# Moving half of the sample-state updates of each mLSTM head into the next head

## The reference, cut to what matters

```
num = einsum(s, v) + w_inter * einsum(q, c_st)          # each of the 4 tokens reads the old memory
den = sum(s) + w_inter * einsum(q, n_st)
h   = num / max(|den|, exp(-m_t))
c_new = decay * c_st + einsum(w_row, k, v)              # the memory that is written back
hn  = (h - mean(h)) * rsqrt(var(h) + EPS)               # per-head norm
out = (hn + skip * xc) * silu(z)
```

## Time and profile before

| | us |
|---|---|
| median of three runs | 1763.48 |
| the profiled execution's own time | 1764.59 |
| its span | 1762.6 |
| TensorE busy in it | 1609.9 (91%) |
| VectorE busy | 665.3 (38%) |
| ScalarE busy | 389.7 (22%) |
| GpSimd busy | 221.7 (13%) |
| DMA, mean over the span | 103 GB/s |

### The profile page before, as it was taken

How to read it: one execution, slowest core, us unless ns; L and a number is a source line. 1 busy time by engine, 2 the same in 40 slices (tenths; PEclk the granted TensorE clock), 3 DMA queues, 4 the chain that set the end, 5 groups by cost and what they waited for, 6 DMA issues and landing times. The chain is left out here.

```text
span 1762.6 us, 22229 instructions
## 1 busy us (share of the span) xinstructions
PE 1609.9 (91%) x8553; PEld 1084.1 (62%) x8553; DVE 665.3 (38%) x1418; ACT 389.7 (22%) x916; POOL 221.7 (13%) x293
## 2 busy tenths in 40 slices
PE   6998598989898699997995999999899999999987
PEld 5886264646464598443444998894347775477752
DVE  1542225555454731005113222032205762176624
ACT  3211131313141321004002221210003331133202
POOL 4010040303030000000003110000201112011120
PEclk9998888989999799998997999959999999999999
DMA  5110027474747622123824240021312211222011
GB/s 161 56 41 0 5 90 244 149 256 145 250 159 242 233 96 103 56 95 125 264 73 135 88 138 1 5 96 48 94 59 97 73 30 52 92 77 77 3 67 51
DMA packets 92639, 181.89 MB, mean 103 GB/s; under 512 B 9927, under 2 KB 23907, under 8 KB 91331
## 3 DMA queue, kind: packets, MB, share of 16 engines
q1 hardware_dynamic: 89286, 163.76, 27.6%
q0 software_dynamic: 3248, 16.72, 2.9%
HBM read 133.82 MB, written 54.95 MB: 107 GB/s over the span
## 5 line engine op out<-in xcount | busy, mean ns | idle before, releaser
L1112 PE MATMUL ps<-wring,xnT 128*128 128x512 f32 (+2 forms) x464 | 177.9, 546 | 0.0
L1112 PEld LDWEIGHTS ps<-wring,xnT 128*128 128x128 f32 (+1 forms) x464 | 83.3, 196 | 97.0 <-issue 96.9
L347 PE MATMUL ps<-xnT,wring 128*128 128x288 f32 (+1 forms) x512 | 120.6, 397 | 1.2 <-PEq L2395 1.2
L1112 PE MATMUL ps<-wring,xcT 128*128 128x512 f32 x256 | 110.9, 594 | 0.0
L347 PEld LDWEIGHTS ps<-xnT,wring 128*128 128x128 f32 x512 | 98.0, 193 | 20.9 <-ACT xnT L268 1.3
L884 DVE SCALAR_TENSOR_TENSOR wring<-wring,nbw,ps 128x512 f32<-128x512 f32 x128 | 86.7, 742 | 63.3 <-PE ps L635 62.1
L2033 ACT ACTIVATE P<-ps,nmx 128x128 f32<-128x128 f32 (+3 forms) x128 | 67.3, 527 | 168.1 <-DVE nmx L2057 167.1
L1932 PE MATMUL ps<-KT,Qp 128*128 128x128 f32 (+3 forms) x256 | 96.5, 459 | 0.0
L2057 DVE TENSOR_REDUCE nmx<-ps 128x1 f32<-128x128 f32 (+3 forms) x128 | 62.0, 486 | 85.2 <-PE ps L1933 84.9
L1112 PEld LDWEIGHTS ps<-wring,xcT 128*128 128x128 f32 x256 | 48.3, 190 | 62.6 <-issue 62.6
L1997 PE MATMUL ps<-V,PT 128*128 128x64 f32 x640 | 85.1, 265 | 0.0
(11 more groups left out here) (434 smaller groups left out, 2755.7 us busy)
## 6 DMA issues: line engine op xcount, KB each, us to landing
wring<-in_state_C_dram SPq DMA_DIRECT2D x32, 1024.0 KB, 6.0
out_dram<-wring SPq DMA_DIRECT2D x32, 1024.0 KB, 5.6
wring<-in_a_w_up_dram SPq DMA_DIRECT2D x8, 2048.0 KB, 8.9
wring<-in_b_w_in_dram SPq DMA_DIRECT2D x8, 2048.0 KB, 8.2
wring<-in_a_w_down_dram SPq DMA_DIRECT2D x4, 2048.0 KB, 7.8
craw<-in_cache_kv_dram SPq DMA_DIRECT2D x64, 128.0 KB
arena<-in_cache_kv_dram SPq DMA_DIRECT2D x32, 256.0 KB, 3.8
arena<-in_cache_win_dram SPq DMA_DIRECT2D x8, 1024.0 KB, 4.9
```

Source lines behind the costliest of these rows:

```text
L347: m = pe.matmul(b[:, 0:t1 - t0], w[:, kt, 128 * m4:128 * m4 + 128], k.xnT[:, kt, t0:t1], start=kt == 0, stop=kt == KD - 1)
L1112: m = pe.matmul(b[0:n, 0:w.shape[2]], xT[:, 8 * half + kt, 128 * i:128 * i + n], w[:, kt, :], start=half == 0 and kt == 0, stop=half == ha ...
```

## The change: what it does

States 4 to 7 of a head (`LATE = 4`) are no longer read and updated within the head but in the first part of the next one: state 4 behind the K products, 5 behind the value products, 6 behind the token-major keys, 7 behind the scores. State 3 moves from ahead of the output products to behind the first transposes that follow them. The fold of the samples' reads ("nums") follows state 7 in the next head; the samples' own product goes into `acc` ahead of the first state's read, and their row sums ("dens") behind the fourth memory product. The samples' variance, deviation and norm move accordingly: the deviation behind the fourth memory product's copy on ScalarE, the norm behind the copy of the row sums on VectorE. For this the halves `kS`, `vS` and the decay rows `nbw` get two buffers, used by turns, and GpSimd waits for state 7 of the head before ahead of the spread queries. The last head has no next one: its states 4 to 7 come at the end of the cell. To make room, the scans' two constant rows lie in the second half of the weight ring and are set in `stage_gates` instead of in the input norm. The core of the diff:

```diff
+LATE = 4
-    nbw = sb("nbw", [128, 2 * S + SB])
+    nbws = sb("nbw", [128, 2, 2 * S + SB])
-    kS = sb("kS", [128, AD], F32R)
-    vS = sb("vS", [128, AD], F32R)
+    kSs = sb("kS", [128, 2, AD], F32R)
+    vSs = sb("vS", [128, 2, AD], F32R)
...
 # sample_state, ahead of state 0
+            pe.wait_ge(k.p_ready, 5 * h + 5)
+            pe.matmul(acc[0:S, :], pS[:, :], vt[0:S, NT, :], start=True, stop=False)
...
+    def sum_samples(pe, h):
+        pe.wait_ge(k.num4_ready, h + 1)
+        b, full = open_bank(pe, k, ("nums", h))
+        pe.matmul(b[0:S, :], k.fold[:, :], num4[:, :], start=True, stop=True).then_inc(full, 1)
...
 # TensorE, one head
             turned_products(1)
+            if h: sample_state(pe, h - 1, LATE, LATE + 1)
 ...value products...
+            if h: sample_state(pe, h - 1, LATE + 1, LATE + 2)
             turned_products(0)
 ...token-major keys...
+            if h: sample_state(pe, h - 1, LATE + 2, LATE + 3)
 ...scores...
+            if h:
+                sample_state(pe, h - 1, LATE + 3, SB)
+                sum_samples(pe, h - 1)
 ...memory products with states 0 and 1 of this head...
+            pe.wait_ge(k.prod_ready, h + 1)
+            b, full = open_bank(pe, k, ("dens", h))
 ...the row sums' five matmuls...
             if h:
                 turn_samples(pe, h - 1)
             sample_state(pe, h, 2, 3)
-            sample_state(pe, h, 3, 5)
 ...output products...
             for i in range(NT):
-                if i < SB - 5:
-                    sample_state(pe, h, 5 + i, 6 + i)
+                if i == 1:
+                    sample_state(pe, h, 3, LATE)
                 pe.wait_ge(k.hn_ready, (NT + 1) * h + i + 1)
...
 # after the last head
+        sample_state(pe, AH - 1, LATE, SB)
+        sum_samples(pe, AH - 1)
         turn_samples(pe, AH - 1)
...
 # GpSimd
             pool.wait_ge(k.qw_ready, h + 1)
+            if h:
+                bank, n = k.bank_of[("up", h - 1, SB - 1, HF - 1)]
+                pool.wait_ge(k.bank_full[bank], n)
...
 # ScalarE
             keep_turned(1, kT)
+            if h: mask(h - 1, SB - 2)
 ...values...
+            if h: mask(h - 1, SB - 1)
             keep_turned(0, qT)
 ...exponentials...
-                sample_deviation(h - 1)
+                keep_sums(h - 1)
 ...masks 0 to 2, copies of the memory products...
+            if h:
+                sample_deviation(h - 1)
             mask(h, 3)
             mask(h, 4)
 ...square root of the prompt's variance...
-            for s in range(5, SB):
-                mask(h, s)
+            mask(h, 5)
...
 # VectorE
             dve.tensor_copy(nbw, b[:, 0:2 * S + SB]).then_inc(free, 1)
+            if h: new_states(h - 1, LATE, LATE + 2)
 ...keys, halves...
-                sample_variance(h - 1)
+                new_states(h - 1, LATE + 2, LATE + 3)
 ...masked scores...
-                sample_norm(h - 1)
+                new_states(h - 1, LATE + 3, SB)
+                keep_sums(h - 1)
+                sample_variance(h - 1)
             new_states(h, 0, 2)
 ...normaliser sums...
+            b, free = full_bank(dve, k, ("dens", h))
+            st.then(dve.tensor_copy(sden[:, :], b[0:S, 0:1]))
             if h:
+                sample_norm(h - 1)
                 mix(h - 1, NT)
             new_states(h, 2, 3)
-            new_states(h, 3, 5)
 ...the prompt's norm...
             for i in range(NT):
-                if i < SB - 5:
-                    new_states(h, 5 + i, 6 + i)
+                if i == 1:
+                    new_states(h, 3, LATE)
                 mix(h, i)
...
 # stage_gates, GpSimd
+        st.then(pool.memset(k.scan_mul[:, :], 1.0))
+        st.then(pool.memset(per_seq(k.scan_mul[:, T:TA])[:, :, 0:1], 0.0))
+        st.then(pool.memset(k.scan_add[:, :], 0.0))
+        pool.memset(per_seq(k.scan_add[:, T:TA])[:, :, 0:1], -1.0e38).then_inc(k.scan_ready, 1)
 # stage_gates, VectorE, ahead of the first scan
+        dve.wait_ge(k.scan_ready, 1)
```

More of the change, by code:

```diff
@@ L628, in sample_state @@
                 m = pe.matmul(acc[32 * ft:32 * ft + 32, :], qm[:, ft, s, :], cs[:, u % NCS, ft, :],
-                              start=s == 0, stop=s == SB - 1)
+                              start=s == 0 and ft > 0, stop=s == SB - 1)
             if s == SB - 1:
@@ L704, in _ @@
             n.then_inc(sums_full, 1)
+            pe.wait_ge(k.prod_ready, h + 1)
+            b, full = open_bank(pe, k, ("dens", h))
+            for ft in range(HF):
+                pe.matmul(b[0:S, 0:1], prod[:, ft, :], k.ones[:, 0:1], start=ft == 0, stop=False)
+            pe.matmul(b[0:S, 0:1], pS[:, :], k.ones[0:S, 0:1], start=False, stop=True).then_inc(full, 1)
             if h:
@@ L817, in sample_deviation, with keep_sums @@
             act.activation(rr[0:S, 2, 0:1], rr[0:S, 1, 0:1], ACT.Sqrt).then_inc(k.sd_ready, 1)
+        def keep_sums(h):
+            act.wait_ge(k.acc_full, h + 1)
+            act.activation(num4[:, :], acc[:, :], ACT.Copy).then_inc(k.acc_free, 1)
+            act.wait_ge(k.acc_free, h + 1)
+            act.sem_inc(k.num4_ready, 1)
         for h in range(AH):
@@ L831, in _ @@
                     for b2 in range(2):
-                        act.activation(vS[32 * b2:32 * b2 + 32, :], b[0:n, :], ACT.Copy)
+                        act.activation(vSs[32 * b2:32 * b2 + 32, h % 2, :], b[0:n, :], ACT.Copy)
                 act.activation(vt[0:n, i, :], b[0:n, :], ACT.Copy).then_inc(free, 1)
@@ L865, in _ @@
             act.activation(rr[:, 2, :], rr[:, 1, :], ACT.Sqrt).then_inc(k.sd_ready, 1)
-            for s in range(5, SB):
-                mask(h, s)
[L868 to L871, removed]
+            mask(h, 5)
+        mask(AH - 1, SB - 2)
+        mask(AH - 1, SB - 1)
+        keep_sums(AH - 1)
         sample_deviation(AH - 1)
@@ L894, in mix, with keep_sums @@
             m.then_inc(free, 1)
+        def keep_sums(h):
+            b, free = full_bank(dve, k, ("nums", h))
+            st.then(dve.tensor_copy(hn_of(h)[0:S, 0, :], b[0:S, :]))
+            dve.sem_inc(free, 1)
         def sample_variance(h):
@@ L916, in _ @@
             b, free = full_bank(dve, k, ("nw", h))
-            dve.tensor_copy(nbw[:, :], b[:, 0:2 * S + SB]).then_inc(free, 1)
+            nbw = nbws[:, h % 2, :]
+            dve.tensor_copy(nbw, b[:, 0:2 * S + SB]).then_inc(free, 1)
             drained(dve, k, ("nw", h))
+            if h:
+                new_states(h - 1, LATE, LATE + 2)
             for i in range(NT + 1):
@@ L925, in _ @@
                 dve.wait_ge(k.km_ready, SB * h)
-            rows = kw[0:S, NT, :]
+            rows, kS = kw[0:S, NT, :], kSs[:, h % 2, :]
             dve.tensor_copy(kS[64:96, :], rows).then_inc(k.ks_ready, 1)
@@ L998, in _ @@
                 dve.tensor_copy(nprow[:, :], b[0:16, 128:256]).then_inc(free, 1)
[L1000 to L1005, removed]
+        new_states(AH - 1, LATE, SB)
+        keep_sums(AH - 1)
         sample_variance(AH - 1)
@@ L2391, in build @@
         with ExitStack() as mlstm:
-            k.scan_add = sb("scan_add", [AH, TA], where=mlstm)
-            k.scan_mul = sb("scan_mul", [AH, TA], where=mlstm)
+            k.scan_add = k.wring[0:AH, 1, 0:TA]
+            k.scan_mul = k.wring[0:AH, 1, TA:2 * TA]
             k.headsel = sb("headsel", [AH, AH, 128], where=mlstm)
```

29 lines of the change are left out of this document (20 added, 9 removed).

## The result

The changed kernel took 1772.84 us (median of 5 runs, 1772.34 to 1774.51) against 1763.22 for the kernel before (5 runs, 1762.29 to 1764.52): ratio 1.0057 [1.0042, 1.0072], slower by about 10 us. The forecast was 1770.4; the measured time lies in its range of 1760.5 to 1779 and in the likeliest case's own, 1764 to 1776. The profiled execution took 1772.34 (span 1770.6, 8.0 more than before's). E is, as in the prediction, the end of a head's output products.

A forecast was written before the change was run, and what follows sets the result against it. TensorE was taken to bound a head, DMA the end behind the last. Fourth head's end 10.0 us earlier, gate weights 16.9 later behind it: +6.9 on 1763.48, so 1770.4 us; range 1760.5 to 1779, likeliest case 1764 to 1776.

The forecast's parts named there:

- The first head: mLSTM cell, first head: without older states, its output products end at 290.2 instead of 297.52.
- The gates stage's memsets: Scan constants now set in the gates stage: covered by VectorE's wait for ScalarE, no cost; without cover 2 us at most.
- A later head: mLSTM cell, heads after the first: 88.1 us between ends of output products, against 89.09; least 85.8, most 92.4.
- E to K's end: Output products' end to last K group: 17.7 us, paced by VectorE; least 16.9, all at half clock 20.3.
- New wait 1: Samples' normalisation behind the last memory product: TensorE idle 2.3 us a head, plus 1.5 at low clock (bounds 0 to 1.7).
- New wait 2: GpSimd waits for the last older state before spreading the queries: no cost taken, up to 1 us a head if late.
- The most for a head: Upper bound for a later head: 66.6+3.8+1.7+20.3=92.4 us.
- the price of L947: Samples' norm on VectorE: 0.53 us; some 0.7 longer if GpSimd's skip products still ran there, which was left out.
- The end: Behind the last head, a chain of stores and loads: gate weights 38.7 us after output products, not 21.8; 16.9 later (13.6 to 19).
- The clock stays up: Rival, chance 0.34: TensorE stays at 2.4 GHz, a head costs 85.8 us, sum 0, 1763.5 us; not slower.
- The clock stays down: Rival, chance 0.14: TensorE's low clock lasts, 90.9 us a head, 8.4 more in all, 1779 us.
- The spreading doesn't do what it says: Rival, chance 0.06: a state's load still comes late in each head, 4.3 x 3 more, 1783 us.

The follow-up runs named there:

- x2: Changed kernel, with the samples' transposes behind state 2's work instead of ahead, VectorE's mix behind its update: 1758.7 us, ratio 0.9978 against the kernel before.
- x6: Changed kernel, with state 3 one place earlier, ahead of the first transposes behind the output products: 1772.04 us, ratio 1.0058 against the kernel before.
- x1: Changed kernel, but the last head does its own eight states within itself, in their old places: 1761.38 us, ratio 0.999 against the kernel before.
- x3: Changed kernel, with state 3 read and updated ahead of the output products, as before the change: 1765.3 us, ratio 1.0014 against the kernel before.
- x5: Changed kernel without the stores of the last head's states 3 and 4: 1765.66 us, ratio 1.0018 against the kernel before.
- x8: Changed kernel, with the samples' root ahead of the memory products' copies on ScalarE: 1769.08 us, ratio 1.0025 against the kernel before.
- x7: Changed kernel with samples' transposes behind state 2 and state 3 ahead of the output products: 1758.31 us, ratio 0.9967 against the kernel before.
- x4: Changed kernel with samples' transposes behind state 2, state 3 ahead of output products, last head doing its own eight states: 1751.29 us, ratio 0.9927 against the kernel before.

## Why the prediction was right

**The first head.** 290.2 was forecast for its E and 288.69 measured; 1.4 of that is a cell that began earlier (first value products at 231.85, before 233.23). From there it is 56.8 against 57.0. The gates stage's memsets (0.54, 0.10, 0.54 and 0.10 us, over at 209.60) cost nothing, as said: VectorE still waits 2.69 for ScalarE there, until 212.27.

**A later head.** 88.1 was forecast, 88.15, 88.45 and 88.6 measured. K's end to E: 70.4 forecast, 71.2 measured (305.62 to 376.84); E to K's end 17.7 and 16.9 (376.84 to 393.77). New wait 1 was 2.30 exactly, built from the same links. Its low clock was undersized: 1.5 with bounds of 0 to 1.7, against 2.4 by x2. The bound counted only the state behind the wait, but the four transposes (0.63 for 0.43) and the first pair of output products (1.75 for 1.12) ran at the low level too. E to K's end came nearer its least, 16.9, than I put it: TensorE was back at full clock ahead of the broadcasts (the last ten matmuls of L671 in 2.70 us), and VectorE paced it, which x6 shows. The two errors, 0.9 too little and 0.8 too much, nearly cancel, so the head's 88.1 is so close partly by luck. New wait 2 cost nothing. The most for a head, 92.4, seems to count the low clock behind wait 1 twice, in 3.8 (2.3 + 1.5) and in 1.7, where the rival's 90.9 has it once; nothing was decided by it.

On the price of L947 the profile after has one row (count, ns min, median and max):

```profile
L947 DVE TENSOR_SCALAR arena<-arena,mv,rr x4: 533/534/534, 360.3 to 593.8; 32x512 f32<-32x512 f32 x4
```

where L911 took up to 1235. In the second head GpSimd's skip products were over at 345.84, long before, so the 0.7 did not arise. But the prediction laid that price at the wrong work: in the kernel before, the long L911 stands beside GpSimd's head blocks (L140), not beside the skip products (L794).

```profile
342.43 3.04 POOL L140 TENSOR_TENSOR bd<-wraw,mask 128x512 f32<-128x512 f32 x3
344.52 1.24 DVE L911 TENSOR_SCALAR arena<-arena,mv,rr 32x512 f32<-32x512 f32 x1
```

Beside the skip products (in the last head, 520.63 to 527.30) L911 took 0.65, at 521.90, and L909 just ahead of it 0.15, as alone; beside the head blocks L909 took 0.93. The Trainium skill, SBUF — State Buffer, Who interferes with whom, says that a VectorE instruction with two SBUF inputs and a GpSimd instruction that reads SBUF shut each other out, and so do one in a two-port mode and any of GpSimd's; which comes second waits for the first to end. The rows beside the head blocks agree; L909's 0.15 beside the skip products, which read SBUF too, does not, by the profile's spans, and the measurement decides. The change moved this conflict: the samples' variance now runs beside the head blocks, and in the second head three of its steps (L936, L938, L939) took 1.02, 0.78 and 0.65 us instead of 0.15 each. It is over at 340.27, long before the root at 359.75, and cost nothing.

**The end.** The weights at E+40.9 against E+38.7 forecast, 19.1 later than before instead of 16.9, at the far bound of 19. The chain was the one forecast, link by link, with other sizes:

| link | forecast | measured |
|---|---|---|
| state 4 done, behind E | 17.3 | 17.4 |
| its store | 5.3 | 7.4 |
| state 7's load | 6.8 | 6.4 |
| reading, update, last store | 9.2 | 9.7 |

The term that was mis-sized most is state 4's store: 5.3 was taken from a store that went out 2.7 us behind a load, and here it went out 1.2 behind one. TensorE idled 5.7 and 5.0 us ahead of the last two states, where about 4 and 6 were forecast. x1 shows that this stretch carries the loss, x3 and x5 that it is this chain. From the weights' load to the end the profiles have 1176.2 us before and 1175.9 after: what follows shifted with it, as said.

**The sum.** -10.0 + 16.9 was forecast, -10.7 + 19.1 = +8.4 measured at the weights, +8.0 in the span and +9.6 by the medians. Without the cell's earlier start the profile would say 9.7 (362.9 - 353.2).

**The rivals.** *The clock stays up* was to decide at 87.0 us a head: no later head came below 88.1. x2 shows that its price was right in kind: with the samples' wait hidden and the clock up behind it, the rival would have had 84.5 (85.8 - 1.3), and x2's heads take 83.6. *The clock stays down* needed 90.9, and TensorE was back at full clock before K's end. *The spreading doesn't do what it says* falls with the rows of L636's waits: no load is late within the heads.

## What to carry to other kernels

Work that is handed from one iteration to the next is handed to nobody by the last one: price the tail as a serial chain (store, load, compute, store), and let the last iteration keep the old order if that chain sets the end. When a stall is taken away, look at which wait is behind it; here a short normalisation took its place, and putting one independent unit of work between its last input and its consumer (x2) was worth 4.8 us a head, where the change itself had won 0.6 ((267.0 - 265.2) / 3, first to fourth E). Price an idle stretch of TensorE with everything that runs at the low clock behind it, not with the first instruction alone.

## What was not expected of the hardware

The clock. A wait of 1.56 us behind small matmuls (x8) was followed by work at the low level as one of 2.30 was; with 0.18 (x2) the clock stayed at 1.00. And in x7 and x4 the same 4.1 us of idle time with the same work behind it was followed by a low stretch that ended with the transposes in one head and lasted to K's end in another. What decides between the two is open; no run here separates it.

Stores beside loads. A store of one state took 5.3 us when it went out 2.7 behind a load, 7.4 at 1.2 behind, 7.9 at 0.85 behind (x8) and 8.6 at 0.53 behind (x1). From the load's issue to the store's end it is 8.1 to 9.2 in these four. It is not a rule: in x1 another store went out 0.53 behind its load, at 548.14, and took 9.9. With no load beside it a store took 4.2 (x3).
